# Decoder step with PEER experts: block 1's queries before tile 1's output projection, attention units on other steps, one VectorE pass for mask, scale and maximum

## What is computed

```python
mp = token_mixer(rms_norm(xp), pos_p, ...)          # sliding-window GQA with sinks, and a gated MLP
xp = xp + mp
xp = xp + memory_attention(rms_norm(xp), mk, mv, w_cq, w_co)
xp = xp + peer_ffn(rms_norm(xp), w_pq, sub_keys, u_tab, v_tab)

def sink_attention(q, k, v, qpos, kpos, sinks):
    s = q . k * HEAD_DIM ** -0.5
    s = where(valid, s, NEG_INF)
    m = maximum(max(s, axis=-1), sink)
    p = exp(s - m)
    probs = p / (sum(p, axis=-1) + exp(sink - m))
    return probs . v

def peer_ffn(x):                                    # per token and head, 8 heads
    s1, i1 = top_k(q1 . keys1, 16); s2, i2 = top_k(q2 . keys2, 16)
    top, sel = top_k(s1[:, None] + s2[None, :], 16) # 16 of 256 pairs
    idx = (i1 * 128 + i2)[sel]; gate = softmax(top)
    a = gelu(x . u_tab[idx]) * gate
    return a . v_tab[idx]                           # 16 rows of 1024 from each table
```

## Time and profile before

| | us |
|---|---|
| median of 3 runs | 1712.26 (1711.76 to 1715.82) |
| the profiled execution | 1714.94 |
| its span | 1713.1 |
| DVE / PE / ACT / POOL busy, share of the span | 68% / 76% / 47% / 38% |
| 576 gathers, bytes | 604.28 MB of 657.35 MB |
| mean rate of all DMAs | 384 GB/s |

### The profile page before, as it was taken

One profiled execution on the slowest core, in us unless ns is written; L12 is line 12 of the kernel. 1 busy time (PEld: TensorE's weight loads), 2 busy tenths in 40 slices (PEclk: granted clock), 3 DMA queues, 4 the chain that ended last, 5 costly groups with the idle time before them and its releaser, 6 DMA issues.

```text
span 1713.1 us, 21597 instructions
## 1 busy us (share of the span) xinstructions
PE 1299.1 (76%) x7069; PEld 470.7 (27%) x7069; DVE 1172.3 (68%) x2765; ACT 811.8 (47%) x2338; POOL 655.0 (38%) x584
## 2 busy tenths in 40 slices
PE   9999868787888776668877676766767667777665
PEld 4455523343443321213222111111111121111110
DVE  2444577887667767777777777777666677677664
ACT  1534356776445455445555454555444445444433
POOL 0000134344444444345445444444444444444441
PEclk9999988898999988889889888788898887787866
DMA  9533699999999999999999999999999999999995
GB/s 349 171 128 143 243 373 422 374 397 399 421 421 421 421 417 407 392 408 419 421 420 420 421 421 422 420 422 421 420 421 421 421 405 421 422 420 421 421 421 219
DMA packets 99041, 657.35 MB, mean 384 GB/s; under 512 B 12576, under 2 KB 17568, under 8 KB 22368
## 3 DMA queue, kind: packets, MB, share of 16 engines
q0 software_dynamic: 83056, 604.28, 85.5%
q1 hardware_dynamic: 15872, 51.68, 8.0%
HBM read 652.71 MB, written 4.19 MB: 383 GB/s over the span
## 4 chain that ended last, share of the span: by engine, by line
DMA 44%; PE 24%; DVE 12%; ACT 11%; issue 7%; SPq 1%; POOL 1%; ACTq 0%; DVEq 0%; POOLq 0%
DMA R<-in_peer_uv,R 42%; PE ps L1982 9%; PE ps L1527 4%; DVE R L1446 4%; PE ps L1499 3%; PE ps L1786 3%; ACT L900 2%; ACT R L909 2%; ACT R L904 2%; DMA R<-in_mem_prompt 1%; ACT L814 1%; ACT R L900 1%; DVE R L1274 1%; DVE R L1275 1%; DVE R L1277 1%
## 5 line engine op out<-in xcount | busy, mean ns | idle before, releaser
L1982 PE MATMUL ps<-R 64*64 64x512 f32 x4544 | 739.6, 732 | 387.0 <-ACT R L909 386.3
L629 POOL DMA_INDIRECT R<-in_peer_uv,R x568 | 644.3, 1134 | 952.2 <-PE ps L1982 765.5
L1446 DVE CUSTOM_DVE_ANT_0 R<-R 128x1024 f32<-128x1024 f32 x568 | 690.7, 1225 | 371.3 <-DMA R<-in_peer_uv,R 364.9
L900 ACT ACTIVATE R<-R 128x1 f32<-128x1 f32 x576 | 115.9, 201 | 606.6 <-DVE R L1446 605.1
L1982 PEld LDWEIGHTS ps<-R 64*64 64x64 f32 x4544 | 135.9, 150 | 739.9 <-ACT R L909 648.9
L909 ACT ACTIVATE R<-R 128x64 f32<-128x64 f32 x576 | 200.4, 348 | 53.2 <-ACT R L904 0.4
L1786 PE MATMUL ps<-A,R 128*128 128x256 f32 (+1 forms) x640 | 221.8, 470 | 0.7 <-ACT R L790 0.7
L904 ACT ACTIVATE R<-R 128x1 f32<-128x1 f32 x576 | 169.8, 295 | 20.9
L1786 PEld LDWEIGHTS ps<-A,R 128*128 128x128 f32 (+1 forms) x640 | 93.4, 197 | 263.8 <-issue 261.3
L1527 PE MATMUL ps<-A,R 128*128 128x512 f32 (+1 forms) x256 | 101.5, 548 | 0.0
L1499 PE MATMUL ps<-R 128*128 128x256 f32 (+2 forms) x384 | 91.6, 393 | 1.5 <-DMA R<-in_w_out 1.5
(11 more groups left out here) (287 smaller groups left out, 909.4 us busy)
## 6 DMA issues: line engine op xcount, KB each, us to landing
R<-in_peer_uv,R POOLq DMA_INDIRECT x568, 15.3
A<-in_w_pq SPq DMA_DIRECT2D x8, 1024.0 KB, 10.1
A<-in_w_in SPq DMA_DIRECT2D x3, 2048.0 KB, 20.8
R<-in_w_out SPq DMA_DIRECT2D x5, 1024.0 KB, 9.7
x_res<-in_x_prompt SPq DMA_DIRECT2D x6, 512.0 KB, 9.4
R<-in_w_out SPq DMA_DIRECT2D x1, 3072.0 KB, 9.9
R<-in_x_promptT SPq DMA_DIRECT2D x4, 512.0 KB, 7.7
R<-in_w_cq SPq DMA_DIRECT2D x2, 1024.0 KB, 10.2
```

The costliest lines, as they stand in the source:

```text
L629: pool.indirect_dma_start(slots[slot_of[g]], None, I["peer_uv"][:, :], bass.IndirectOffsetOnAxis(ap=idx[:, b % 4, k:k + 1], axis=0)).then_ ...
L900: act.activation(hgelu[:, b % 2, col], hdot[:, b % 2, col], ACT.Gelu).then_inc(gelu_ready, 1)
L1446: dve.tensor_tensor_reduce(u, u, xn(t), 1.0, 0.0, ALU.mult, ALU.add, hdot[:, b % 2, k:k + 1]).then_inc(u_used, 1)
L1982: ins = pe.matmul(bank(2 * (t % 2) + q)[rows], diag[tokens, g % DIAGS, :], v_rows[slot_of[g]][tokens, c * 512:(c + 1) * 512], start=first, ...
```

## The change

In the prologue PE makes block 1's queries first, and puts their transposes and scores between the matmuls of tile 1's output projection (`out_one`). ACT and DVE follow: ACT takes the queries out around `gates(0, 0)`, DVE does both `top_keys` of block 1 before the first expert step, and adds the projection into x in step 0 (`add_one`). ACT's Square for tile 1's cross norm moves into the loop (`PREP_AT[1]` from -1 to 1). The units move to 24, 33, 39, 45, 51, 57; the steps of the row norms move with `norm_step`; ACT's `gates` stands behind the units in an iteration. Tile 3's rows get a place of their own (`attn_out_of`). Slot 5 enters at 14 instead of 13, slot 9 stays until 66 instead of 60. Block 12's queries start one step earlier and take two of PE's steps at once (`QUICK`), so that `experts_of(12)` stands at g = 183 instead of 188. On DVE a unit's scale, mask and maximum are four instructions of 256 columns in place of three of 512, 512 and 1024.

```diff
-SLOT_PHASES = ((0, (0, 9, 1, 2, 3, 4)), (13, (0, 9, 1, 2, 3, 4, 5)), (31, (0, 1, 2, 3, 4, 5, 7, 9)),
-               (60, (0, 1, 2, 3, 4, 5, 7)), (140, (0, 1, 2, 3, 4, 5)), (225, (0, 1, 2, 3, 4, 5, 6)), (278, tuple(range(9))))
+SLOT_PHASES = ((0, (0, 9, 1, 2, 3, 4)), (14, (0, 9, 1, 2, 3, 4, 5)), (31, (0, 1, 2, 3, 4, 5, 7, 9)),
+               (66, (0, 1, 2, 3, 4, 5, 7)), (140, (0, 1, 2, 3, 4, 5)), (225, (0, 1, 2, 3, 4, 5, 6)), (278, tuple(range(9))))
...
-        PREP_AT = {1: -1, 2: 122, 3: 200, 4: 210}
-        QUERY_AT = {1: 5, 2: 134, 3: 208, 4: 218}
-        CROSS_AT = {1: 8, 2: 138, 3: 222, 4: 244}
+        PREP_AT = {1: 1, 2: 123, 3: 200, 4: 210}
+        QUERY_AT = {1: 6, 2: 134, 3: 208, 4: 218}
+        CROSS_AT = {1: 9, 2: 138, 3: 222, 4: 244}
...
-        UNIT_AT = (22, 29, 36, 43, 50, 57)
+        UNIT_AT = (24, 33, 39, 45, 51, 57)
...
+        LATE = {4: 8, 12: 7}
+        QUICK = (12,)
...
+                if s in QUICK and 0 <= d < KD // 2:
+                    steps += [(s, 2 * d), (s, 2 * d + 1)]
+                elif s in QUICK and KD // 2 <= d < 2 * TOPK:
+                    steps.append((s, d + KD // 2))
...
+        def norm_step(t, part):
+
+            return (12, 15, 17, 20)[part] if t == TILES - 1 else (16, 18, 21, 24)[part]
...
             scores_out(0)
             act.wait_ge(gvn_out, TILES)
             act.activation(mv_l, mv, ACT.Copy).then_inc(mv_moved, 1)
+            queries_out(1)
             gates(0, 0)
+            queriesT_out(1)
+            scores_out(1)
...
-            prep(1, 0)
-            queries_out(1)
-            queriesT_out(1)
-            scores_out(1)
...
-                elif step == 13 and r == 1:
+                elif step == norm_step(t, 0) and r == 1:
                     act.wait_ge(a_o, 2 * (t - 1))
...
-            dve.wait_ge(wo_done, 3)
-            dve.tensor_tensor(xr(1), xr(1), ps[:, 1024:2048], ALU.add).then_inc(x1_out, 1)
+            for c in range(2):
+                top_keys(1, c)
+
+            def add_one():
+
+                dve.wait_ge(wo_done, 3)
+                dve.tensor_tensor(xr(1), xr(1), ps[:, 1024:2048], ALU.add).then_inc(x1_out, 1)
...
-                    over = band[:, :].unsqueeze(1).broadcast_to([P, 2, 2 * P])
-                    dve.scalar_tensor_tensor(U_s[:, 0:2, :], v3(bank(2), 2), 0.125, over, ALU.mult, ALU.add)
-                    dve.scalar_tensor_tensor(U_s[:, 2:4, :], v3(bank(3), 2), 0.125, over, ALU.mult, ALU.add).then_inc(a_sc, 1)
-                    dve.wait_ge(a_sc, u + 1)
                     if u > 0:
                         dve.wait_ge(a_exp, u)
+                    for i in range(4):
+                        ins = dve.tensor_tensor_reduce(U_s[:, i, :], v3(bank(2 + i // 2), 2)[:, i % 2], band[:, :], 0.125,
+                                                       LOWEST, ALU.add, ALU.max, mx[:, 4 + i:5 + i])
+                    ins.then_inc(a_sc, 1)
+                    dve.wait_ge(a_sc, u + 1)
                     sk = v3(sinks[:, :], 2)[:, :, 2 * r:2 * r + 2]
-                    chain(dve.tensor_reduce(mx[:, 4:8], U_s, AX_X, ALU.max))
...
+                    if g == 0:
+                        add_one()
...
-            for c in range(2):
-                product(bank(2 + c), lambda k: T1[:, k, :], lambda k: w_out[:, 2 * c:2 * c + 2, k, :]).then_inc(wo_done, 1)
-            q_mm(1)
+            out_one(0, 0, 2)
             q_T(1)
+            out_one(0, 2, 4)
             scores(1)
+            out_one(0, 4, KD)
+            out_one(1, 0, KD)
...
-                    if r == 1:
-                        pe.wait_ge(n_T, t - 1)
+                    if u == 4:
+                        pe.wait_ge(n_T, 2)
```

More of the change, by code:

```diff
@@ L930, in _ @@
                             scores_out(n)
-                        if step == 21:
-                            gates(n, n % 4)
                     if k == 9 and b in FINAL_SLOT:
@@ L939, in _ @@
                         unit(t, r, u, g - at)
+                    for n, step in query_steps(g):
+                        if step == 21:
+                            gates(n, n % 4)
                     for t in PREP_AT:
@@ L1394, in unit @@
                     dve.wait_ge(a_pv, u + 1)
-                    if t > 2 and r == 0:
-                        dve.wait_ge(n_tr, t - 1)
+                    if t == 3 and r == 0:
+                        dve.wait_ge(pq_q, 4)
+                    if t == 4 and r == 0:
+                        dve.wait_ge(n_tr, 2)
                     if u == 0:
@@ L1403, in unit @@
                     ins.then_inc(a_o, 1)
-                elif step == 15 and r == 1:
-                    attn_scaled(t, OU)
-                elif step == 20 and r == 1:
+                elif step == norm_step(t, 1) and r == 1:
+                    attn_scaled(t, attn_out_of(t))
+                elif step == norm_step(t, 3) and r == 1:
                     attn_take(t)
@@ L1447, in _ @@
                     for n, step in query_steps(g):
-                        if n == 1 and step in (16, 17):
-                            top_keys(1, step - 16)
                         if n > 1 and step in (14, 15):
@@ L1825, in _, with out_one @@
             scores(0)
+            q_mm(1)
             pe.wait_ge(n_T, 1)
             pe.wait_ge(h_T, 4)
-            for c in range(2):
-                product(bank(2 + c), lambda k: T1[:, k, :], lambda k: w_out[:, 2 * c:2 * c + 2, k, :]).then_inc(wo_done, 1)
-            q_mm(1)
+            def out_one(c, first, end):
+                for k in range(first, end):
+                    ins = pe.matmul(bank(2 + c), T1[:, k, :], w_out[:, 2 * c:2 * c + 2, k, :], start=(k == 0),
+                                    stop=(k == KD - 1))
+                if end == KD:
+                    ins.then_inc(wo_done, 1)
+            out_one(0, 0, 2)
             q_T(1)
+            out_one(0, 2, 4)
             scores(1)
+            out_one(0, 4, KD)
+            out_one(1, 0, KD)
             def prep(t, step):
@@ L1954, in unit @@
                     ins.then_inc(a_pv, 1)
-                elif step == 17 and r == 1:
-                    pe.wait_ge(a_pTo, 2 * min(u + 2, 6))
-                    attn_T(t, OU, bank(6))
+                elif step == norm_step(t, 2) and r == 1:
+                    pe.wait_ge(a_pTo, 2 * min(u + 3, 6))
+                    if t == TILES - 1:
+                        pe.wait_ge(n_T, t - 1)
+                    attn_T(t, attn_out_of(t), bank(6))
             def out_piece(n):
```

22 lines of the change are left out of this document (17 added, 5 removed).

## The result

The change made the kernel slower. Six runs each gave a median of 1725.10 us (1721.20 to 1728.28) against 1715.09 (1711.76 to 1717.69). The ratio is 1.0061, 95% interval 1.0043 to 1.0079: 10.5 us more, where 12 less were forecast. The profiled execution took 1721.20 us, the fastest of its six; its span is 1719.4, so the two traces show 6.3 us of the 10.5.

What follows compares the result with a forecast made beforehand. From the first gather on, the DMA engines (421 GB/s) were taken as the bound. Savings of 3.8 (start), 6.4 (attention units) and 2.8 (block 12), 13.0 us, took 1712.3 to 1699.3, stated as 1700; range 1694 to 1710.

Steps and rivals of the forecast that it cites:

- The start: 205 to 250 us: block 1's queries inside the projection bring the seventh gather 3.5 us earlier; 3.8 us saved.
- Block 12: 720 to 725 us: earlier indices remove POOL's wait of 7.11 us for DVE; 2.8 of 2.9 us saved.
- The fused pass: DVE's scale, mask and maximum in the attention units: 1.9 us a unit for 2.6, 4 us in six.
- The loads: ACT's table loads among the attention units: 18 for 26, 1.29 us a change, 10.3 us of ACT saved.
- Of 9.5 us lost I take 6.4 as regained, two thirds: Attention units, 315 to 350 and 380 to 405 us: 6.4 us of empty DMA time regained; bounds 9.5 and none.
- Both get lighter just there: At 315 and from 380 us, the late engines get lighter: ACT by 10.3 us, DVE by 4.
- The DMA engines have 8 slots, 20 us of data, to bridge such delays: Attention units: 20 us of queued data covers longer ACT visits and slots delayed some 1.6 us at five places.
- The eighth slot stays for six steps more, until 65: Attention units: the slot kept for six more steps covers the stretch from 380 us.
- From there on both traces run at 421 GB/s: After block 12: same rate and same work left, so the end moves by the sum of the earlier savings.
- Rival 3: Attention units: three-load visits at steps 28, 49, 61, 69 drain the slots, 5.4 us each; slower, 1717.8; chance 0.09.
- sign of error: Among the attention units: DMA at under 350 GB/s behind an ACT visit with three loads.
- rival 1: Attention units keep their 9.5 us loss because ACT's longer visits give back the saved loads; 1705.7; chance 0.17.

Runs made afterwards that it cites:

- the start alone: Kernel before with only the prologue reorder, tile 1's cross norm in the loop and slot 5 from step 14: ratio 0.9995.
- the first kernel: The change with attention units, row norms and gates in their old places: ratio 0.9952; with block 4's queries doubled for earlier indices, 0.9978.

## Why the prediction was wrong

- *The start, 3.8 us.* The steps held: the new order on PE, the issues of slots 3 and 4, DVE's wait (2.07 us) and its second step 10.2 us after the first gather (forecast 10.3). The seventh gather won 2.5 us, not 3.5. In the end 0.9 us is left, with an interval that holds 0. The term was too large; 215 to 250 us ran at 392 GB/s in the changed kernel, not at over 410, and with the start alone its window won 1.5 us. I also looked at one window and not at what follows it, and of "slot 5 enters at 14 instead of 13" I priced nothing, though it moves the last steps of slots 7 and 9.
- *Block 12, 2.8 us.* Right: 3.1 by itself.
- *The fused pass.* Right in kind, a little better in size: 1.4 us a unit for 1.9, 3.9 us of time by itself. The halved rate of the Trainium skill ("Vector Engine (DVE) Microarchitecture Reference", Points that are easy to get wrong) is not seen in this pass. But the page speaks of two sources in SBUF and one is in PSUM here, so the pass does not test it: a pass of 256 columns takes 0.42 us, as the plain one.
- *The loads.* 18 as counted, 1.28 us each. Where a load was taken from a late visit it was worth about its length (5.5 us for four). The Trainium skill's 2.66 us each ("ScalarE: Activation LUTs", What ACT_TABLE_LOAD costs) would make it 10.6; the runs go with the rows.
- *"Of 9.5 us lost I take 6.4 as regained, two thirds".* **This is the step that failed.** With the fused pass the stretch's part came to 18.7 - 3.9 = 14.8 us lost. The two sentences that carried it fell. "Both get lighter just there" summed up the busy time of two engines; both did get lighter (ACT 59.4 us of busy time in 315 to 405, was 67.1), and the time rose. "The DMA engines have 8 slots, 20 us of data, to bridge such delays" took the slots for a reserve that is full when a visit comes. In the trace PE, DVE and POOL stay late past the visit, the indices of block 4 come at 382.67 us, and the DMA engines run dry (29 GB/s in 380 to 385). That the places cost it is shown: the old ones give 14.2 us back. How the 14.2 divide among the visits is not. I had written down the warning, for step 28: a visit just ahead of `scores_out(3)`. The same stood at step 49 ahead of `scores_out(4)`, and I did not look.
- *"The eighth slot stays for six steps more, until 65".* Wrong: its last step is 59, as my own sentence on x_res had it. The order of gathers, not the phase table, says when a slot is used.
- *"From there on both traces run at 421 GB/s".* Not quite: 725 to 1690 us lost 4.6 us more by the rates, a term that I had put at nothing. Its cause stays open.
- *The rivals.* Rival 3 (three-load visits drain the slots, 1717.8, chance 0.09) was the right one in sign and nearly in mechanism: 350 to 405 us, at and behind the visits of steps 49 and 61, runs at 341 and 311 GB/s, as its sign of error said (though the lowest rate, in 380 to 385 us, stands behind the wait for indices and ahead of the second visit). Its price of 5.4 us a visit is not what was found. No single visit has a fixed price: places made 14.2 us, the third loads 5.5, of which most is the loss that earlier indices take away too. Its chance was too low: against it I set only that today's visit met a queue of others close together, and against its neighbour, rival 1, that ACT's total falls. Neither says what is due behind a visit.

## What to carry to other kernels

When work is regrouped to save table loads, don't add up busy time: for every place where an engine leaves the main loop, list what is due on the other engines in the next three to five steps, and what waits for that in turn. A queue of buffers can hide one delay, but a chain back to the address producer (here ACT, PE, ACT, DVE, POOL) can let the queue run dry long after, as it did here. Time each part of a bundled change by itself: here two of four parts were clearly good, one brought nothing that stands clear of the noise, and the fourth hid them.

## What the runs showed that I had not expected

- PE after 4.12 us without work did its first step in 1.98 us instead of 1.09, so a pause costs more than its length just when PE has fallen behind.
- Removing a wait of POOL for indices of 8.00 us lost 4.5 us in one kernel, and removing one of 9.96 us won 9.4 in another. The length of a wait before a DMA issue says little by itself; look at where the pause turns up instead. In the first kernel PE, no longer busy, stood still for 4.09 us at ACT's visit and fell to the lower clock.
- One step's shift in a least-recently-used slot rotation moved two other slots' last use by 7 and by 6 steps, and made a second number in the same table without effect.
